# Masks by TensorE, later transposes, mem_v between output units, memory probabilities scaled from PSUM

## What is computed

```python
def diff_attn_group(p, lam_q1, lam_k1, lam_q2, lam_k2, subln_w, lam_init):
    ...
    for qb in range(S // Q_BLOCK):
        qs, qe = qb * Q_BLOCK, (qb + 1) * Q_BLOCK
        mask = (jnp.arange(qe) // CHUNK)[None, :] <= (jnp.arange(qs, qe) // CHUNK)[:, None]
        s1 = jnp.einsum("bqhd,bkhd->bhqk", q1[:, qs:qe], k1[:, :qe]).astype(f32) * scale
        s2 = jnp.einsum("bqhd,bkhd->bhqk", q2[:, qs:qe], k2[:, :qe]).astype(f32) * scale
        p1 = jax.nn.softmax(jnp.where(mask, s1, NEG_INF), axis=-1)
        p2 = jax.nn.softmax(jnp.where(mask, s2, NEG_INF), axis=-1)
        attn = (p1 - lam * p2).astype(v.dtype)
        outs.append(jnp.einsum("bhqk,bkhd->bqhd", attn, v[:, :qe]))

def memory_cross_attn(hn, memn, w_mq, w_mk, w_mv, w_mo):
    ...
    s = jnp.einsum("bshd,bmhd->bhsm", q, k).astype(jnp.float32) * (MEM_HEAD_DIM ** -0.5)
    pr = jax.nn.softmax(s, axis=-1).astype(v.dtype)
    o = jnp.einsum("bhsm,bmhd->bshd", pr, v).reshape(B, S, D_MODEL)
    return o @ w_mo

def first_block(...):
    ...
    h = h + jnp.concatenate([y_rwkv, y_diff], axis=-1) @ w_out[l]
    h = h + memory_cross_attn(rms_norm(h, norm_mem_w[l]), rms_norm(mem, norm_src_w[l]),
                              w_mq[l], w_mk[l], w_mv[l], w_mo[l])
```

## Time and profile before

| | |
|---|---|
| median of 3 runs | 2298.88 us (2295.61 to 2299.90) |
| the profiled execution | 2298.79 us, its span 2297.0 us |
| TensorE busy | 2154.6 us, 94% of the span, 13158 matmuls |
| GpSimd busy | 1190.1 us, 52% |
| VectorE busy | 1051.2 us, 46% |
| ScalarE busy | 598.3 us, 26% |
| mean granted clock of TensorE | 0.978 |
| differential attention | 169 to 233 us |
| output and mem_v units | 404 to 492 us |
| memory attention | 504 to 585 us |

### The profile page before, as it was taken

The page is one execution under the profiler, slowest core; times in us unless marked ns, Lnnn a source line. Parts: engine busy times, 40 slices in busy tenths (PEclk is TensorE's granted clock), DMA queues, the critical chain, the costliest instruction groups (busy, mean ns, idle before and its releaser), DMA issues.

```text
span 2297.0 us, 31733 instructions
## 1 busy us (share of the span) xinstructions
PE 2154.6 (94%) x13158; PEld 1741.5 (76%) x13158; DVE 1051.2 (46%) x1452; ACT 598.3 (26%) x1185; POOL 1190.1 (52%) x660
## 2 busy tenths in 40 slices
PE   6998788888999999998998999999999989999999
PEld 4775677777888888875676788888877767888887
DVE  6886545724532022465997642023335665320320
ACT  2234434212321021113334321012135552210210
POOL 4661004662566666652432366666654435666665
PEclk9998899999999999998999999999999999999999
DMA  5321001231233333321211133333322212333332
GB/s 192 92 74 37 3 22 56 83 106 48 68 92 101 93 99 94 99 83 46 65 56 46 46 92 97 95 100 93 101 78 69 63 39 83 92 101 93 100 94 90
DMA packets 49658, 182.58 MB, mean 79 GB/s; under 512 B 5504, under 2 KB 5632, under 8 KB 49280
## 3 DMA queue, kind: packets, MB, share of 16 engines
q1 hardware_dynamic: 49248, 179.10, 25.9%
q10 hardware_dynamic: 288, 1.77, 0.2%
HBM read 178.75 MB, written 2.10 MB: 79 GB/s over the span
## 4 chain that ended last, share of the span: by engine, by line
PE 83%; DVE 11%; issue 2%; ACT 2%; POOL 1%; DMA 0%; SPq 0%; ACTq 0%; DVEq 0%; POOLq 0%
PE PB L1614 23%; PE PB L1615 23%; PE PB L1617 23%; PE PB L1578 10%; DVE AR L899 4%; PE PB L1671 2%; ACT AR L418 2%; PE PB L1581 2%; DVE AR L902 1%; DVE HN L902 1%; DVE AR L906 1%; DVE SM L1377 1%; DVE SM L933 1%; DVE AR L1380 1%; POOL WL L409 1%
## 5 line engine op out<-in xcount | busy, mean ns | idle before, releaser
L1615 PE MATMUL PB<-AR_r,WL 128*128 128x512 f32 (+1 forms) x2520 | 969.7, 386 | 0.0
L407 POOL TENSOR_SCALAR WH<-W 128x1024 fp32r<-128x1024 f32 x328 | 354.5, 1081 | 1069.0 <-PE PB L1617 784.7
L409 POOL TENSOR_TENSOR WL<-W,WH 128x1024 fp32r<-128x1024 f32 x328 | 835.8, 2548 | 27.3
L1617 PE MATMUL PB<-AR_r,WH 128*128 128x512 f32 (+1 forms) x2520 | 610.1, 384 | 0.0
L1615 PEld LDWEIGHTS PB<-AR_r,WL 128*128 128x128 f32 x2520 | 478.0, 190 | 98.7 <-issue 5.5
L1617 PEld LDWEIGHTS PB<-AR_r,WH 128*128 128x128 f32 x2520 | 466.5, 188 | 93.5
L1614 PE MATMUL PB<-AR_r,WH 128*128 128x512 f32 (+1 forms) x1304 | 494.7, 383 | 4.7 <-POOL WL L409 4.7
L1614 PE MATMUL PB<-HN_r,WH 128*128 128x512 f32 x1216 | 490.1, 403 | 0.6 <-POOL WL L409 0.4
L418 ACT ACTIVATE AR<-AR 128x512 f32<-128x512 f32 (+4 forms) x278 | 161.0, 616 | 753.6 <-DVE AR L902 667.5
L1578 PE MATMUL PB<-AR 64*64 64x64 f32 (+5 forms) x4736 | 262.3, 257 | 45.6 <-issue 13.3
L902 DVE SCALAR_TENSOR_TENSOR AR<-PB,AR 128x512 f32<-128x512 f32 (+3 forms) x153 | 98.9, 646 | 417.8 <-PE PB L1617 365.0
(11 more groups left out here) (103 smaller groups left out, 1043.4 us busy)
## 6 DMA issues: line engine op xcount, KB each, us to landing
W<-weights_in SPq DMA_DIRECT2D x328, 512.0 KB, 3.6
C<-constants_in SPq DMA_DIRECT2D x1, 2784.0 KB, 16.4
H<-x_in SPq DMA_DIRECT2D x4, 512.0 KB, 6.8
h_out<-H SPq DMA_DIRECT2D x8, 256.0 KB, 4.6
AR<-mem_in ACTq DMA_DIRECT2D x1, 1024.0 KB, 4.9
V<-vectors_in ACTq DMA_DIRECT2D x1, 703.0 KB, 4.4
C<-constants_in SPq DMA_DIRECT2D x1, 68.0 KB, 3.2
```

The lines of the kernel that those rows point to most:

```text
L407: pool.tensor_scalar(WH[:, u % 2, :], w, 1.0, 1.0, ALU.mult, ALU.mult).then_inc(sems["w_round"], 1)
L409: pool.tensor_tensor(WL[:, u % 2, :], w, WH[:, u % 2, :].bitcast(F32), ALU.subtract)\
L1615: pe.matmul(out, ll, rh, start=False, stop=False)
L1617: ins = pe.matmul(out, lhs(k)[0], rhs(k)[0], start=False, stop=stop and k == KT - 1)
```

## The change

The same values are computed. In the differential attention the mask is no longer added by VectorE but by a second matmul of TensorE, identity times `chunk_bias`, into the last 64 columns of each score map. The transposes are four steps behind the scores and the value product five; PR1 has a fourth plane; ScalarE takes Exp ahead of the copy of the transposes; and TensorE's value units stand right behind the scores of their round. Ahead of the memory attention, five mem_v units stand between output units and three behind the last (OUT_AT, MEM_V_AT; the fetches follow), their evictions between VectorE's steps, their banks are MV_BANK's, and their transposes come at the end, around `norm_sum`. In the memory attention Exp is written back to its PSUM bank, and VectorE's scaling reads it there and writes to MPR; the bank is free for the next scores only after the scaling.

```diff
+OUT_AT, MEM_V_AT = (0, 1, 3, 5, 7, 9, 11, 12), (2, 4, 6, 8, 10, 13, 14, 15)
+for _n in range(8):
+    FETCH[UNIT["out"] + OUT_AT[_n]] = UNIT["out"] + _n
+    FETCH[UNIT["out"] + MEM_V_AT[_n]] = UNIT["mem_v"] + _n
...
-        PR1, PR2 = ([AR[:, a, :] for a in planes] for planes in ((15, 16, 17), (18, 19, 20)))
+        PR1, PR2 = ([AR[:, a, :] for a in planes] for planes in ((15, 16, 17, 39), (18, 19, 20)))
...
-        PIPE, LAG = 3, 4
+        PIPE, LAG = 3, 5
...
+        MV_BANK = (7, 4, 7, 4, 7, 0, 1, 2)
...
             for i in range(len(steps) + LAG + 1):
-                if 3 <= i < len(steps) + 3:
-                    tr_evac("diff", i - 3, steps[i - 3][1] + 1)
                 if i < len(steps):
                     w = (steps[i][1] + 1) * P
                     act.wait_ge(sems["sc_max"], i + 1)
                     if i >= 3:
-                        act.wait_ge(sems["tr_mm"], i - 2)
+                        act.wait_ge(sems["prob"], i - 2)
+                    if i >= 4:
+                        act.wait_ge(sems["tr_mm"], i - 3)
...
                     value_tokens_ev(i // 2)
+                if 4 <= i < len(steps) + 4:
+                    tr_evac("diff", i - 4, steps[i - 4][1] + 1)
...
-            rstd(N_MEM, "eps1")
-            for m in range(8):
+
+            def mem_tokens_ev(m):
                 act.wait_ge(sems["vt_tr"], VT["mem"] + m + 1)
                 f(MV[:, :, tile(m)], PB[5 + m % 2][:, 0:MEM].rearrange("p (t n) -> p t n", t=2), ACT.Copy).then_inc(*A.inc("ev_act"))
+            for m in range(5):
+                mem_tokens_ev(m)
+            rstd(N_MEM, "eps1")
+            for m in range(5, 8):
+                mem_tokens_ev(m)
...
                     act.wait_ge(sems["sc_max"], b + i + 1)
-                    if i >= 2:
-                        act.wait_ge(sems["tr_mm"], b + i - 1)
-                    f(MPR[:, i % 2, 0:MEM], PB[4 + i % 2][:, 0:MEM], ACT.Exp, bias=nmax(i), accum_out=psum_of(i))\
+                    f(PB[4 + i % 2][:, 0:MEM], PB[4 + i % 2][:, 0:MEM], ACT.Exp, bias=nmax(i), accum_out=psum_of(i))\
...
                     banks = [PB[4 + 2 * (i % 2)], PB[5 + 2 * (i % 2)]]
-                    for pb in banks:
-                        tt(pb[:, w - 64:w], pb[:, w - 64:w], cst("chunk_bias"), ALU.add).then_inc(*D.inc())
-                    dve.wait_ge(*D.latest)
...
-            split_residual(N_MEM, "out", lambda k: k % 4, "mem", lambda k: vec("norm_mem", k, k + 1), RL, ACC)
-            for m in range(8):
+            split_residual(N_MEM, "out", lambda k: k % 4, "mem", lambda k: vec("norm_mem", k, k + 1), RL, ACC, at=OUT_AT,
+                           between=lambda k: mem_value(k - 2) if 2 <= k < 7 else None)
+            for m in range(5, 8):
                 mem_value(m)
...
-                    ts(MPR[:, j % 2, 0:MEM], MPR[:, j % 2, 0:MEM], recip(j), None, ALU.mult).then_inc(*D.inc("prob"))
+                    if j >= 2:
+                        dve.wait_ge(sems["tr_mm"], BASE["mem"] + j - 1)
+                    ts(MPR[:, j % 2, 0:MEM], PB[4 + j % 2][:, 0:MEM], recip(j), None, ALU.mult).then_inc(*D.inc("prob"))
...
-                        last = mm(PB[b][:, 0:w], DQ[r, h, tile(t)], DK[r, h, 0:w])
+                        mm(PB[b][:, 0:w], DQ[r, h, tile(t)], DK[r, h, 0:w], stop=False, skip_group_check=True)
+                        last = mm(PB[b][:, w - 64:w], cst("ident"), cst("chunk_bias"), start=False, skip_group_check=True)
...
-            project(8, 0, "norm_h", "out", first="unit", evbase=RES[N_MEM])
...
+            for i in range(16):
+                if i in OUT_AT:
+                    k = OUT_AT.index(i)
+                    project(1, k % 4, "norm_h", "out", first=False if k else "unit", evbase=RES[N_MEM] + k)
+                else:
+                    m = MEM_V_AT.index(i)
+                    project(1, MV_BANK[m], "vt_ev", "src", first=False, width=MEM, evbase=VT["mem"] + m, banks=8)
+                    if m == 5 or m == 6:
+                        mem_tokens(2 * m - 10)
+                        mem_tokens(2 * m - 9)
+            mem_tokens(4)
+            norm_sum(N_MEM)
+            for m in range(5, 8):
+                mem_tokens(m)
...
-                    free[b] = ("sc_exp", EXPB["mem"] + i + 1)
+                    free[b] = ("prob", b0 + i + 1)
```

More of the change, by code:

```diff
@@ L524, in _ @@
                     if i >= 3:
-                        act.wait_ge(sems["tr_mm"], i - 2)
+                        act.wait_ge(sems["prob"], i - 2)
+                    if i >= 4:
+                        act.wait_ge(sems["tr_mm"], i - 3)
                     for m, pr in enumerate((PR1, PR2)):
-                        f(pr[i % 3][:, 0:w], PB[4 + 2 * (i % 2) + m][:, 0:w], ACT.Exp, bias=nmax(i, m), accum_out=psum_of(i, m))\
+                        f(pr[i % (4, 3)[m]][:, 0:w], PB[4 + 2 * (i % 2) + m][:, 0:w], ACT.Exp, bias=nmax(i, m), accum_out=psum_of(i, m))\
                             .then_inc(*A.inc("sc_exp"))
@@ L933, in rd, with split_residual @@
                 return dve.tensor_reduce(out, in_, AX.X, op, negate=negate)
-            def split_residual(n, unit, bank, x, w, sq, acc, per=1):
+            def split_residual(n, unit, bank, x, w, sq, acc, per=1, at=None, between=None):
                 base = SPLIT_NO[x] * KT
@@ L939, in split_residual @@
                     if k < KT:
-                        dve.wait_ge(sems["w_used"], UNIT[unit] + per * (k + 1))
+                        dve.wait_ge(sems["w_used"], UNIT[unit] + (per * (k + 1) if at is None else at[k] + 1))
                         tt(H[:, k, :], H[:, k, :], PB[bank(k)][:, :], ALU.add).then_inc(*D.inc("norm_h"))
+                    if between is not None:
+                        between(k)
                     if k:
@@ L1064, in _ @@
                     w = (steps[j][1] + 1) * P
-                    p1, p2 = PR1[j % 3][:, 0:w], PR2[j % 3][:, 0:w]
+                    p1, p2 = PR1[j % 4][:, 0:w], PR2[j % 3][:, 0:w]
                     dve.wait_ge(sems["sc_exp"], 2 * (j + 1))
@@ L1204, in mem_value @@
             def mem_value(m):
-                dve.wait_ge(sems["w_used"], UNIT["mem_v"] + m + 1)
-                tt(MV[:, :, tile(m)], PB[m % 4][:, 0:MEM].rearrange("p (t n) -> p t n", t=2), RSS.rearrange("p (t n) -> p t n", t=2),
+                dve.wait_ge(sems["w_used"], UNIT["out"] + MEM_V_AT[m] + 1)
+                tt(MV[:, :, tile(m)], PB[MV_BANK[m]][:, 0:MEM].rearrange("p (t n) -> p t n", t=2), RSS.rearrange("p (t n) -> p t n", t=2),
                    ALU.mult).then_inc(*D.inc("vt_ev"))
@@ L1735, in _ @@
                         free[b] = ("sc_exp", 2 * (i + 1))
-                if 3 <= i < len(steps) + 3:
-                    j = i - 3
+                if i in (1, 3, 5):
+                    value_unit((i + 1) // 2)
+                if i in (1, 3, 5, 6):
+                    value_tokens(i // 2)
+                if 4 <= i < len(steps) + 4:
+                    j = i - 4
                     pe.wait_ge(sems["prob"], j + 1)
@@ L1740, in _ @@
                     for k in range(steps[j][1] + 1):
-                        last = tr(PB[0][:, tile(k)], PR1[j % 3][:, tile(k)])
+                        last = tr(PB[0][:, tile(k)], PR1[j % 4][:, tile(k)])
                         if k == steps[j][1]:
@@ L1758, in _ @@
                         free[b] = ("od_ev", h + 1)
-                if i in (1, 3, 5):
-                    value_unit((i + 1) // 2)
-                if i in (1, 3, 5, 6):
-                    value_tokens(i // 2)
             alpha, beta = (lambda p, t: KK[:, p, tile(t)]), (lambda p, t: AG[:, p, tile(t)])
@@ L2023, in _, with mem_tokens @@
             evb = 26
-            project(8, 0, "norm_h", "out", first="unit", evbase=RES[N_MEM])
-            for m in range(9):
-                if m < 8:
-                    project(1, m, "vt_ev", "src", first=False, width=MEM, evbase=VT["mem"] + m)
-                if m == 0:
-                    take(4)
-                    norm_sum(N_MEM)
-                if m:
-                    to_tokens(5 + (m - 1) % 2, lambda t: MV[:, t, tile(m - 1)], VT["mem"] + m - 1, evb + m, 2)
+            def mem_tokens(m):
+                to_tokens(5 + m % 2, lambda t: MV[:, t, tile(m)], VT["mem"] + m, evb + m + 1, 2)
+            for i in range(16):
[12 more added lines that the diff above has]
+                mem_tokens(m)
             project(2, 6, "mq_ev", "mem", first="unit", banks=8)
```

## The result

| | before | changed |
|---|---|---|
| median of 18 runs each, us | 2296.7 | 2306.6 |
| lowest to highest, us | 2291.0 to 2305.6 | 2299.3 to 2309.8 |
| profiled execution, its span, us | 2298.8, 2297.0 | 2308.6, 2306.8 |

The ratio is 1.0037, 95% interval 1.0028 to 1.0047. The forecast was 2289.9 us, its range ended at 2296.

What follows compares the result with a forecast made beforehand. TensorE, busy 94% of the span, was taken as the bound, with gains only where it waits or runs slowly. -8.1 + 1.5 - 2.3 = -8.9 from 2298.8 gave 2289.9 us; forecast 2284 to 2294.3 (73%), full range 2283 to 2296.

Steps and rivals of the forecast that it cites:

- part 3: Differential attention, masks moved to TensorE and transposes and value products later: -2.3 us, bounds -6.5 to +4.
- part 2: Ahead of the memory attention, mem_v units between output units: +1.5 us, bounds -4 to +4.
- part 1: Memory attention, scaling read from PSUM so that it no longer waits for GpSimd's splitter: -8.1 us, bounds -10.5 to -5.
- no 6 us wait: Mixed units: TensorE's 6.00 us wait for the sum of squares ahead of the memory attention was to go.
- half of a spell's 1.6: +0.8: Mixed units' end: TensorE idles 2.9 us, and half of a possible lower-clock spell was counted, +0.8 us.
- score 0.76, mask 0.4: Differential attention, full heads: TensorE times in a dependence loop of 5.0 us for two steps, 10.0 a head.
- masks of 8 steps: +3.2: Differential attention, first seven steps: TensorE's added mask products were to cost +3.2 us, at 0.4 a step.
- The last rival: TensorE at its lower clock from the second value unit to the differential attention's end: +17.7 us, 2309.9 in all; 3%.
- score 7: Differential attention: this score was to start near 199.5 us, 4.7 us before its earlier 204.18.
- The twelve instructions that took 1.48 us: Differential attention: 128-column products at about 0.11 us each, used to price a step's four mask instructions at 0.4 us.
- Heads of 10 to 10.5 us: Differential attention: sign to look for, a full head taking 10 to 10.5 us, 10.5 before.
- a mask above 0.15 us an instruction: Differential attention: sign that its change would end above zero.

Runs made afterwards that it cites:

- e1: The kernel before with only the differential attention's change (masks on TensorE, transposes and products a step later, copies behind Exp); 2304.4 us.
- e11: The kernel before with only the mem_v units moved between the output units; 2302.2 us.
- e7: The kernel before with only the memory attention's change (Exp written back to PSUM, scaling read from there); 2288.6 us.
- e2: The kernel before with the memory attention from PSUM and mem_v between output units, differential attention untouched; 2294.3 us.
- e9: e8 without the mixed units: eight output units, then the mem_v units, as in the kernel before; 2277.6 us.
- e8: e4 with ScalarE's copies of the transposes ahead of Exp instead of behind it; 2281.8 us.
- e3: The changed kernel with both scores of a step first, then both masks; 2291.7 us.
- e6: The kernel before with later transposes and value products, copies behind Exp and the fourth plane, masks still added by VectorE; 2292.5 us.
- e4: e3 with each mask product on only the 64 rows of its own map; 2286.5 us.
- e12: e8 with the four products in the changed kernel's order (score, mask, score, mask), masks still on 64 rows; 2280.1 us.
- e5: The kernel before with the mask products alone, in the order score, mask, score, mask, VectorE's additions gone; 2305.3 us.

## Why the prediction was wrong

The forecast was -8.9 us, the measurement +9.9, 18.8 more. By the parts' own runs, part 3 came out 10.7 us above its forecast (e1), part 2 4.3 above (e11), part 1 0.5 (e7). These three sum to 15.5. The other 3.3 us no run shows: the medians of the parts alone add up to +6.6 (-7.6 + 5.8 + 8.4).

**Part 1: right.** Forecast -8.1; the stretch gave -8.1, e7's median -7.6. The scaling from PSUM took 0.485 us in the changed kernel, where the prediction had 0.42; query waits fell to 0.7 (0.6 forecast), L906's to 2.0 in all (1.3 forecast).

**Part 2: right in its mechanism, too small in size.** Units of 4.28 us (4.3), no 6 us wait, 2.65 us for ScalarE (2.9). From the first output unit to the first query unit the changed kernel took 88.1 us, as before; the sum for that was +0.7. The rest of the 1.5 us in the trace is half clock in the query units behind it (+1.4 us where "half of a spell's 1.6: +0.8" was forecast). But in the medians the part costs more: e11 +5.8, from e7 to e2 +5.9, from e9 to e8 +4.3, each against its own before, the last with overlapping intervals. B shows 2.1 to 3.5 of them. Where the other 1 to 4 us fall I can't show. In D, kernels with the part had 314.1 to 319.0 in six traces of seven, those without it 311.5 to 314.4 in seven; that is suggestive and no more. The prediction let nothing change behind the memory attention; the rows of D don't bear that out. (Half of 5.44 is 2.7, not 2.9, but the row is right: 24 short matmuls 0.12 us apart take 2.9.)

**Part 3: wrong.** Forecast -2.3 (bound +4) against the profiled execution of before; measured +9.7 against the same execution, +8.4 in e1's median, +13.1 with the clock's part taken out. The step that failed is the loop of a full head, "score 0.76, mask 0.4", and with it "masks of 8 steps: +3.2". 0.76 was the mean of a pair of scores as they stood in before, and I took it over as if the edit left it alone. Parted, the two take 2 x 1.05 at 512 columns and 2 x 0.84 at 384 from start to start, about twice the pair. The masks cost 0.37 and 0.24 us, 0.61 a step, where 0.4 was taken and 0.6 was the bound; four in a row, in e3, cost 0.46, so much of that excess comes from the parting too. I also asked only how long the loop of dependences was (10.0 us a head), never how much work TensorE itself had in a head: four products (2.7 us), four transposes and six value instructions (ten at the 0.11 of the earlier trace rows) make 3.8 us for a step of 512 columns, and the head of 13.1 has only 0.77 of waiting in it. That TensorE's own work became the bound was none of my rivals. The last rival's 2309.9 us is near what was measured, but its mechanism, a clock at the lower level to the end of the attention, did not come: the clock was 0.95.

The other terms of part 3 hold. In e6, where the masks stay with VectorE, score 7 begins 27.4 us after the first score (198.01 less 170.63), 35.0 before: -7.6, where the prediction's terms without "masks of 8 steps" give -7.9. Its heads take 10.4 us, the forecast was 10 to 10.5. Its whole stretch is 5.0 us shorter than before's; by the terms without the masks it should be 5.5.

The sign could be read ahead. The twelve instructions that took 1.48 us are eight of a value product, 0.11 us apart, and the next step's four score instructions of 64 rows, which I took for products of the same kind. At the pace of the eight, four of 512 are 4 x 4 x 0.11 = 1.8 us, but the four scores took 1.13, too little for products in a row. The Trainium skill (TensorE: Matmul & The Clock Gate, "Part 3: Packing small matmuls — row/col tiling") has the rule: products whose operands lie in different row groups run concurrently. These traces agree, 1.13 us for two maps against 1.12 for one. The Trainium skill also says in "Key Properties" of TensorEngine Tiling (Array Packing) that a change of tiling mode drains the engine. e3, e4 and e12 fit that, since only the mask on 128 rows between the scores cost the overlap, and so does the mask's own time, 0.37 us with a score of 64 rows behind it and 0.24 with a product of 128. That the overlap was lost by a drain is still not shown: a mask that merely takes both halves of the rows would cost it too.

**What I said would show it.** Score 7 was to start near 199.5 us; its first map began at 204.05 (205.47 less a score and a mask), its second at 205.47, where both had begun at 204.18 before. Heads of 10 to 10.5 us: 13.1. The releaser, ScalarE's copy, was right, but for 4.3 us in all. The sentence that a mask above 0.15 us an instruction puts part 3 above zero came true (0.61 a step are 0.15 for each of four), for a lesser reason than the real one: in e4, with masks of 64 rows, the four take 0.33 us.

**The clock.** Before lost 5.2 us to it in A (65.8 at 0.87 against e2's 60.6 at 1.00), not the 8 that the prediction works out from length times missing clock. TensorE was busy only 55.0 of the 65.8 us, and a slower matmul can use up a wait; that this makes the difference is argued and not measured. The changed kernel had 0.95 there, so the clock did improve, by less than the parted scores cost.

## What to carry to other kernels

Before an instruction is put between two matmuls, look whether these two run side by side: operands on different rows of the array, and a time for both that is no longer than for one. A mask, a bias or a correction put in between should use the same rows as the product that it corrects; here the scores side by side again took 11.3 us off (e1 to e3), masks on the rows of their own map another 2.7 in A (e3 to e4), and only the copies ahead of Exp, 7.0 more (e4 to e8), made it a clear gain. And for each engine that is given work, add up its own busy time for a round next to the chain of waits: the longer of the two is the round.

## What the runs showed of the hardware

- Two float32 matmuls (two instructions each) on rows 0 to 63 and 64 to 127 took 1.13 us together at 512 columns, one alone 1.12. A matmul on all 128 rows between them made them run one after the other (changed kernel, e1, e5); behind both it didn't (e3).
- They need not be neighbours: in e12 the score on the upper rows started ahead of a mask on the lower rows that precedes it in the program. The Trainium skill (the same Part 3) says that matmuls start in program order; this trace disagrees.
- Time and granted clock go together from run to run: the changed kernel's 18 runs went from 2299.3 us at a mean clock of 0.984 to 2309.8 at 0.979. Untouched code (D) took 311.5 to 311.6 us in six traces at 0.95, 314.1 to 314.5 in six at 0.94, 313.0 in one, and 319.0 at 0.91. The first kind, in e1:

```profile
1029.83:1341.32 311.49, 279.86 (x1402) 211.46 (x1400) 238.66 (x410) 110.06 (x220) 114.10 (x64) 0.95 0.18 54
```

One pair of traces can thus differ by 7.5 us where nothing was changed; only stretches at the same clock, or medians of many runs, tell an edit of this size.
